# Seven block products in place of eight for half of an MLP's second projection, with weight sums made by accumulating DMAs

## The reference

```python
def squared_relu_mlp(h, w1, w2):
    return jnp.square(jax.nn.relu(h @ w1)) @ w2      # w1 2048 x 8192, w2 8192 x 2048

x = x + squared_relu_mlp(rmsnorm(x, norm_mlp[l]), w_mlp_in[l], w_mlp_out[l])
```

## Time and profile before

| | |
|---|---|
| median of 3 runs | 1684.41 us (1684.21 to 1684.99) |
| the profiled execution | 1684.11 us |
| its span, first to last instruction | 1682.3 us |
| PE busy, share of the span | 99% |
| DVE, ACT busy | 66%, 47% |
| granted TensorE clock | 1.0 |
| P2, four turns | 382.6 to 1085.9 us of the span |

### The profile page before, as it was taken

The page is one execution under the profiler, slowest core; times in us unless marked ns, Lnnn a source line. Parts: engine busy times, 40 slices in busy tenths (PEclk is TensorE's granted clock), DMA queues, the critical chain, the costliest instruction groups (busy, mean ns, idle before and its releaser), DMA issues.

```text
span 1682.3 us, 25173 instructions
## 1 busy us (share of the span) xinstructions
PE 1673.5 (99%) x9397; PEld 1453.9 (86%) x9397; DVE 1112.0 (66%) x1118; ACT 795.6 (47%) x989; POOL 55.2 (3%) x61
## 2 busy tenths in 40 slices
...
PEclk9999999999999999999999999999999999999999
...
GB/s 310 220 133 110 189 138 175 163 211 269 255 280 251 260 278 277 253 232 279 266 289 243 254 260 256 214 235 168 174 164 177 196 190 188 182 192 174 196 205 88
DMA packets 171692, 361.48 MB, mean 215 GB/s; under 512 B 11008, under 2 KB 17472, under 8 KB 171344
## 3 DMA queue, kind: packets, MB, share of 16 engines
...
q10 hardware_dynamic: 144, 0.26, 0.0%
...
## 4 chain that ended last, share of the span: by engine, by line
PE 97%; DVE 1%; issue 1%; DMA 0%; ACT 0%; SPq 0%; POOLq 0%; POOL 0%; ACTq 0%; DVEq 0%
PE G L762 31%; PE S L762 13%; PE S L776 12%; PE G L776 12%; PE G L745 10%; PE G L779 6%; PE S L779 6%; PE S L715 1%; PE G L751 1%; PE S L1147 0%; DMA raw<-in_w_in 0%; DVE window_sums L1830 0%; PE S L1140 0%; PE S L1126 0%; PE S L1014 0%
## 5 line engine op out<-in xcount | busy, mean ns | idle before, releaser
L1453 DVE TENSOR_TENSOR w_lo<-raw,w_hi 128x1024 fp32r<-128x1024 f32 (+1 forms) x573 | 704.1, 1245 | 416.5 <-ACT w_hi L1181 415.0
L1181 ACT ACTIVATE w_hi<-raw 128x1024 fp32r<-128x1024 f32 (+1 forms) x574 | 591.6, 1046 | 593.1 <-PE G L762 176.7
L762 PE MATMUL G<-w_hi,X_pair 128*128 128x512 f32 (+2 forms) x1456 | 444.5, 383 | 0.1
L762 PEld LDWEIGHTS G<-w_hi,X_pair 128*128 128x128 f32 x1456 | 269.6, 188 | 55.4 <-issue 3.3
L762 PE MATMUL G<-w_lo,X_pair 128*128 128x512 f32 (+2 forms) x728 | 276.8, 380 | 0.0
L776 PE MATMUL S<-Y_pair,w_hi 128*128 128x512 f32 x768 | 267.0, 390 | 0.0
L776 PE MATMUL G<-Y_pair,w_hi 128*128 128x512 f32 x768 | 266.8, 390 | 0.0
L779 PE MATMUL G<-Y_pair,w_lo 128*128 128x256 f32 x768 | 216.6, 282 | 0.0
L779 PE MATMUL S<-Y_pair,w_lo 128*128 128x256 f32 x768 | 216.6, 282 | 0.0
L745 PE MATMUL G<-Y_pair,w_hi 128*128 128x256 f32 x1088 | 194.0, 280 | 1.1 <-DVE Y_pair L1569 0.9
L776 PEld LDWEIGHTS S<-Y_pair,w_hi 128*128 128x128 f32 x768 | 144.2, 188 | 30.2
...
## 6 DMA issues: line engine op xcount, KB each, us to landing
raw<-in_w_in SPq DMA_DIRECT2D x142, 512.0 KB, 4.5
raw<-in_w_mlp_in SPq DMA_DIRECT2D x128, 512.0 KB, 5.3
raw<-in_w_mlp_out SPq DMA_DIRECT2D x128, 512.0 KB, 6.5
ada_w<-in_w_ada SPq DMA_DIRECT2D x64, 768.0 KB, 4.7
raw<-in_w_out SPq DMA_DIRECT2D x64, 512.0 KB, 4.4
raw<-in_w_merge SPq DMA_DIRECT2D x64, 512.0 KB, 4.2
raw<-in_w_branch_attn SPq DMA_DIRECT2D x16, 512.0 KB, 4.4
raw<-in_w_branch_pool SPq DMA_DIRECT2D x16, 512.0 KB, 6.0
```

The source lines that it names most:

```text
L762: ins = nc.tensor.matmul(token_bank(bank, tt)[:, 0:n], a[:, c0 + c, tok], w[:, s % SPLIT, c, 0:n], start=first and c == 0 and k == 0, stop ...
L1181: nc.scalar.activation(w_hi[:, s % SPLIT, :, 0:n], raw[:, k, :, 0:n], ACT.Copy).then_inc(hi_ready, 1)
L1453: nc.vector.tensor_tensor(w_lo[:, s % SPLIT, :, 0:n], raw[:, k, :, 0:n], w_hi[:, s % SPLIT, :, 0:n], ALU.subtract).then_inc(lo_ready, 1)
```

## The change

Half of the down half of each turn, the output columns 0 to 1023, is computed otherwise. The turn's 16 chunks of 128 hidden features form two sets of 8. In each set four chunks (two pairs) are multiplied by the two 512-column blocks with **seven** products of a 128-token half with 256 rows x 512 columns instead of eight (the Winograd form of Strassen's scheme), and the other four chunks as before. A set is 11 sub-blocks: V1 to V7, of 6 matmuls each, and N1A, N1B, N0A, N0B, of 12 each. The order in a set is V1, N1A, V3, N1B, V2, V5, N0A, V6, V7, N0B, V4. So a turn has 70 slots: 32 up, 22 mixed, 16 down. Sub-block 37 is V5 of the first set, 42 its V4, 48 V5 of the second set, and sub-block 54 is the first behind the sets.

The seven products need sums of activations and sums of weights.

- Activations: `sum_x` (4 DVE operations of 128 x 256), `sum_hi` (ACT), `sum_lo` (2 DVE operations of 128 x 512), once for each set.
- Weights: stage `neg{k}_{g}` is one ACT operation that writes the negative of a tile to another buffer (or to the same one), and then a DMA of POOL adds a sub-block of `w_mlp_out` from HBM onto it (`accum_op=ALU.add`). k = 1, 2, 4 form a chain: the negation of 2 starts from the landed sum 1 (semaphore `t1_in`), that of 4 from the landed sum 2 (`t2_in`). V5, V6, V7, V4 convert the sums 1, 2, 3, 4.
- The results are put together by `mixA` (ACT) and `mixB` to `mixG` (two DVE operations each) in place of `down0` and `down1`.

Besides, Relu and Square of the hidden features move from one DVE operation to two ACT operations ahead of the copy to `x_hi` (`hid` is now 3 operations of ACT); `hlo` (the former DVE part of `hid`) has a slot of its own behind it; the ada halves are in slots 0 to 33 (26 halves, thirteen rows) and 55 to 61 (three rows); `ada_fold` is cut in two; SP's part of P2 is unrolled, with 62 raw loads a turn; the sums for the last norm are taken later in the last turn.

```diff
-ADA_OPS = [0, 2, 4, 6, 7, 9, 11, 13, 14, 16, 18, 20, 21, 23, 25, 27, 28, 30, 32, 34, 35, 37, 39, 41, 42, 44, 46, 48,
-           49, 51, 53, 55]
+ADA_OPS = [0, 1, 2, 3, 4, 5, 6, 8, 10, 12, 13, 14, 16, 17, 18, 19, 20, 21, 22, 24, 26, 28, 29, 30, 32, 33,
+           55, 56, 57, 58, 60, 61]
...
+V1, N1A, V3, N1B, V2, V5, N0A, V6, V7, N0B, V4 = range(SET_SUBS)
+NEGATED = [(26, 0, 1), (28, 0, 3), (30, 0, 2), (33, 0, 4), (36, 1, 1), (38, 1, 3), (41, 1, 2), (45, 1, 4)]
...
+for _s in range(UP + SET_SUBS + V6):
...
+    for _j in range(4):
+        if _s == 8 * _j + 7:
+            stage("P2", _s, f"up{_j}", A=1, D=1)
+        if _s == 8 * _j + 8:
+            stage("P2", _s, f"hid{_j}", A=3)
+        if _s == 8 * _j + 9:
+            stage("P2", _s, f"hlo{_j}", D=1)
...
+    for _at, _g, _k in NEGATED:
+        if _s == _at:
+            stage("P2", _s, f"neg{_k}_{_g}", A=1)
...
+            def mixed(s, loop, i, j):
...
+                pe.wait_ge(lo_ready, count(s, loop, 1))
...
+                    elif k in (V1, V2, V4):
+                        ch = 8 * g + (0 if k == V1 else SUB) + c
+                        tok = slice(P, TOK) if k == V4 else slice(0, P)
+                        ins = product(PRODUCT[k], x_hi[:, ch, tok], x_lo[:, ch, tok], c)
+                    else:
+                        m = {V5: 0, V6: 1, V7: 2, V3: 3}[k]
+                        ins = product(PRODUCT[k], x_sum_hi(g, m)[:, c, :], x_sum_lo(g, m)[:, c, :], c)
...
+                elif name[:3] == "neg":
...
+                    else:
+                        act.wait_ge(t2_in, i * 32 + 16 * (g + 1))
+                        from_ = w_added(g, 2)
...
+                    nc.scalar.activation(w_added(g, k), from_, ACT.Copy, scale=-1.0).then_inc(act_side, 1)
...
                     act.wait_ge(dve_side, done("D", f"up{b}", i))
+                    nc.scalar.activation(right[:, :, :], right[:, :, :], ACT.Relu).then_inc(act_side, 1)
+                    act.wait_ge(act_side, step("A", name, 1, i))
+                    nc.scalar.activation(chunked(hid), right[:, :, :], ACT.Square).then_inc(act_side, 1)
+                    act.wait_ge(act_side, step("A", name, 2, i))
                     nc.scalar.activation(x_hi[:, 4 * b:4 * b + 4, :], chunked(hid), ACT.Copy).then_inc(act_side, 1)
...
-                    dve.wait_ge(dve_side, step("D", name, 1, i))
-                    nc.vector.scalar_tensor_tensor(chunked(hid), right[:, :, :], 0.0, right[:, :, :],
-                                                   ALU.max, ALU.mult).then_inc(dve_side, 1)
...
+            def add_to(g, k, i):
+                pool.wait_ge(act_side, done("A", f"neg{k}_{g}", i))
...
+                pool.dma_start(w_added(g, k), t["w_mlp_out"][row0:row0 + P * SUB, NW * n:NW * (n + 1)]
+                               .rearrange("(c p) n -> p c n", p=P), accum_op=ALU.add
+                               ).then_inc({1: t1_in, 2: t2_in, 3: t3_in, 4: t4_in}[k], 16)
```

More of the change, by code:

```diff
@@ L252 @@
         stage("P1", _s + 2, f"out_sq{_n}", A=2)
-for _j in range(4):
-    stage("P2", 8 * _j + 7, f"up{_j}", A=1, D=2)
-    stage("P2", 8 * _j + 8, f"hid{_j}", A=1, D=1)
-stage("P2", 34, "mlp_rms", D=3)
-for _n in range(4):
-    if _n == 3:
-        stage("P2", 58, "ada_fold", D=2)
-    if _n < 3:
-        stage("P2", 39 + 8 * _n, f"down{_n}", D=2)
+stage("P2", 3, "mlp_rms", D=3)
+for _s in range(UP + SET_SUBS + V6):
+    for _g in range(SETS):
+        if _s == 16 * _g + 9:
+            stage("P2", _s, f"sum_x{_g}", D=4)
+        if _s == 16 * _g + 10:
+            stage("P2", _s, f"sum_hi{_g}", A=1)
+        if _s == 16 * _g + 11:
+            stage("P2", _s, f"sum_lo{_g}", D=1)
+    for _j in range(4):
[5 more added lines that the diff above has]
+            stage("P2", _s, f"hlo{_j}", D=1)
+    if _s == UP + SET_SUBS + V1:
+        stage("P2", _s, "mixA", A=1)
+    for _at, _g, _k in NEGATED:
+        if _s == _at:
+            stage("P2", _s, f"neg{_k}_{_g}", A=1)
+    if _s == UP + SET_SUBS + N1B:
+        stage("P2", _s, "mixB", D=2)
+_set = UP + SET_SUBS
+stage("P2", _set + V6, "mixC", D=2)
+stage("P2", _set + V7, "mixD", D=2)
+stage("P2", _set + V4, "mixE", D=2)
+stage("P2", UP + MIXED, "mixF", D=2)
+stage("P2", UP + MIXED + 1, "mixG", D=2)
+stage("P2", 62, "ada_fold0", D=2)
+stage("P2", 63, "ada_fold1", D=2)
+stage("P2", 64, "down2", D=2)
 stage("P2", SPLIT_AT, "down3_0", P=1, D=1)
@@ L838, in loop_waits @@
                         pe.wait_ge(dve_side, step("D", "down3_1", 1, i - 1) if i else done("D", "res_T3"))
-                    if s in (16, 24, 32, 48):
-                        pe.wait_ge(dve_side, step("D", f"up{0 if s == 16 else 1 if s == 24 else 2 if s == 32 else 3}", 1, i))
-                    if b == 4 and s % 2 == 0:
-                        pe.wait_ge(dve_side, done("D", f"hid{(s % 8) // 2}", i))
+                    if s in (16, 24, UP, UP + V2):
+                        pe.wait_ge(dve_side, step("D", f"up{(16, 24, UP, UP + V2).index(s)}", 1, i))
+                    if s == UP + MIXED:
+                        pe.wait_ge(dve_side, done("D", "mixD", i))
+                    if s == UP + MIXED + 8:
+                        pe.wait_ge(dve_side, done("D", "mixG", i))
                 else:
@@ L1177, in main @@
                     return
-                act.wait_ge(raw_in[k], v if loop is None else loop[0] * (16 * loop[1] // RAW) + v)
+                r = raw_of(s, loop)
+                g, k = set_sub(s, loop)
+                if k in SET_SUMS:
+                    act.wait_ge({V5: t1_in, V6: t2_in, V7: t3_in, V4: t4_in}[k], loop[0] * 32 + 16 * (g + 1))
+                else:
+                    act.wait_ge(raw_in[r % RAW], raw_count(r, loop))
                 if s >= SPLIT:
-                    act.wait_ge(used, count(s, loop, 1 - SPLIT))
-                nc.scalar.activation(w_hi[:, s % SPLIT, :, 0:n], raw[:, k, :, 0:n], ACT.Copy).then_inc(hi_ready, 1)
+                    here = s - PHASE["P2"][0]
+                    early = in_mlp(loop) and any(k <= here < k + SPLIT - 1 for k in SKIPS_AT)
+                    act.wait_ge(used, count(s, loop, 1 - (SPLIT - 1 if early else SPLIT)))
+                nc.scalar.activation(w_hi[:, split_of(s, loop), :, 0:n], source(s, loop)[:, :, 0:n], ACT.Copy).then_inc(hi_ready, 1)
             def halves(name, dst, chunks, i=None, gain=None):
@@ L1425, in norm_sums @@
                     else:
-                        act.wait_ge(dve_side, step("D", f"down{n}", tt + 1, last) if n < 3 else step("D", f"down3_{tt}", 1, last))
+                        act.wait_ge(dve_side, done("D", "mixG", last) if n < 2 else step("D", "down2", tt + 1, last) if n < 3
+                                    else step("D", f"down3_{tt}", 1, last))
                     src = x_nf[:, tt, :] if k else x[:, tt, NW * n:NW * (n + 1)]
```

277 lines of the change are left out of this document (241 added, 36 removed).

## The result

The changed kernel takes **1715.99 us** (median of 4 runs, 1713.99 to 1716.52), the kernel before 1684.35: ratio 1.0185, 95% interval 1.0167 to 1.0203. It is slower by 31.6 us, where +5.6 was forecast (1690, range 1679 to 1704). The profiled execution took 1716.03 us, its span 1714.2, which is 31.9 over the span before.

The account below looks back on a forecast made before the run. PE was taken to bound the kernel, busy 99% at clock 1.0. 1684.1 (profiled) - 10.9 (matmuls) + 4 x 3.99 (waits) + 0.5 (hand-overs) = 1689.7; the median 0.3 higher: 1690 us, range 1679 to 1704.

Parts of the forecast that it names:

- The gain: Mixed sets of P2's down halves: 48 matmuls fewer, 10.88 us saved, 2.72 a turn.
- The wait ahead of V5: Once a turn PE waits 3.99 us for sub-block 37, since ACT's neg4_0 can't start before DVE's hlo3 ends.
- Its last leg: From the start of w_lo of sub-block 36 to V5's first product: 6.65 us in the laying-out.
- The accumulating DMAs: POOL's adding DMAs in P2: each lands 6.5 us after issue, so hidden, with little to spare.
- The allowance of 6.8 us: Second set of a turn: three landings and two negations before V4's conversion allow 6.8 us for each landing.
- The slope: Landings beyond 6.9 us: 16 us in all for each us; stated as +12 at 7.5, +20 at 8.0.
- The clock: PE's granted clock in P2: taken as 1.0, with no term for a fall.
- The last turn: Later norm sums of the last turn and the two halves of ada_fold: zero, at most 1 us once.
- `mixC` and `mixD`: They end 0.35 us before PE wants sub-block 54: no cost, but first to go when V4's sum is late.
- ada: Row loads in P2's dense part: 4.7 us each, late only from about 6.5; at 8 a turn grows by 1.2.
- the sums come late: Rival: accumulation of 7 to 8 us, or ada rows of 8, gives 1692 to 1705 us; chance 0.17.
- the doubled transfer: Rival: adding DMAs read two sources and take 11.0 us, giving 1755 us; above 1705, chance 0.10.

Follow-up runs that it names:

- e14: Changed kernel with stages respread over slots, no adding DMAs or negations: plain DMAs bring each sum's second tile, DVE subtracts the first; 1679.82 us, ratio 0.9971.
- e3: Changed kernel with plain copies in place of POOL's adding DMAs, leaving out the adding; 1710.79 us, ratio 1.0154.
- e5: Changed kernel with the negations and adding DMAs of sums 2 and 3 of the first set exchanged; 1724.54 us, ratio 1.0238.
- e11: Changed kernel with stages, POOL's DMAs and ada rows respread, plain copies for adding DMAs; 1679.80 us, against 1694.28 for the same kernel with adding.
- e4: Kernel before, with one PE wait added in each turn's down half, meant as about 4.3 us (turns 0, 2) or 2.4 us (1, 3); 1708.74 us.
- e15: e14 with norm sums in slots 56, 58, 62 instead of 56, 59, 61 and two ada halves one slot earlier; 1679.73 us, ratio 0.9973.
- e13: Changed kernel respread over slots, last turn with sums2 in slot 61, ada_fold in 64 and 66; 1694.49 us, against 1694.28 with sums2 in 62, ada_fold in 66.

## Why the prediction was wrong

The sign and the mechanism ahead of V5 were right; the time was 26 us off. Two steps failed most: the clock, put at 1.0 and so at nothing, where it took about 11 us; and the landings of the adding DMAs, put at 6.5 us each, where they took 6.0 to 13.1. Waits of PE came to 25.3 us instead of 16.5; of what lies beyond 4 x 3.99, late sums made 4.1 (2.1 ahead of V5, 2.0 near the end of the mixed part), the end of the last turn 3.3 and sub-block 36 2.0. By its own steps:

1. **The gain**: forecast 2.72 us a turn. Where nothing waits (e14), a down half takes 84.6 instead of 87.05: 2.45 us, 9.8 in all. Nearly right.
2. **The wait ahead of V5**, 3.99 forecast: 3.96 in turn 0. Its last leg holds where the order alone releases it (6.7 us in e3 and e5, 6.65 laid out). But in all four turns the adding DMA of sum 2 ended last, by 0.3 us in turn 0 and more in the others, and the wait in those was 4.48 to 5.03. Over four turns 18.0 us instead of 16.
3. **The accumulating DMAs**: this term failed. 6.5 us was the median of the 24 into `w_sum` to 0.1, but over all 32 it is 8.9, and a chain isn't made of medians. I took one price for all eight, though in the first set sum 3 is issued 3 us ahead of sum 2: they landed after 10.9 to 12.1 and 12.1 to 13.1 us. The allowance of 6.8 us was worked out for the second set alone; for the first I had not asked when sum 2 must be there. The slope was not in step either: 16 us for each us beyond 6.9 makes +15 at 7.5 and +23 at 8.0, not +12 and +20. The causes are the adding (2 to 3 us of a landing, and 14.5 us of the whole in e11) and the place behind sum 3 in the queue. I had kept the rule of the Trainium skill (page "Collectives: The Full Stack", section "The bandwidth ceiling: the fold count and why AG ≠ RS ≠ AR": a reduction reads two sources and runs at half the rate, stated there for collectives) as a rival. Its direction is borne out by e11: 9.4 against 6.5 us. The sum that I hung on it, 1755, is not: the adding didn't double the landing.
4. **The clock** was assumed at 1.0 without a word, and this was the largest miss. Taking each down half less 84.6 and less its waits leaves 3.2, 3.1, 3.3 and 6.1 us: 15.7 in all. An estimate splits it. PE worked through 23.7 of the 30.7 us at 0.5, with 0.427 us from one matmul to the next instead of 0.227, which loses 11.1 us. Each of the 13 waits costs 0.27 us that the brackets don't count (see the last section), 3.5 us. About 0.9 us of the last turn stands in e14 too. e4 shows the clock's part in the kernel before: 1.9 to 3.0 us on top of each such wait.
5. **The last turn**: "zero, at most 1 us once". It was a wait of 2.52 behind `sums2` with 3.4 us at 0.5, one of 0.79 close ahead of it, and two more of 1.08 (ahead of sub-block 36) and 0.78 (for `mixD`) in that turn.
6. **`mixC` and `mixD`** had 0.35 us of reserve and were "the first to go": PE waited 0.67 and 0.78 us for `mixD` in turns 1 and 3. Right.
7. **ada**: "late only from 6.5 us". The median is 6.4, single rows were later: row 12 took 8.0 to 9.8 us in the changed kernel, where DVE stood up to 2.2 us for it beside the other two chains, and in e3 DVE stood up to 5.2 us for it.

The balance of P2: -9.8 (gain) + 25.3 (all waits of 0.3 us and more) + 15.7 = +31.2, as measured. Since the 15.7 is what was left over, that this agrees proves nothing; the estimate in step 4 is worked out apart from it and gives 15.5. As to the rivals: "the sums come late" (0.17) was the nearest in kind, but at 1692 to 1705 without the clock. With the clock at 1.0 and a median for each landing, no case above 1705 but the doubled transfer was in my list.

What stays open: what decides when in a wait, or behind it, the clock falls (in e4 1.66 us ahead of the end of one wait of 4.30 us and 0.59 behind that of the other), and why some waits up to 3.72 us brought no fall; the 4.7 us that the last down half of e14 loses, of which 3.3 are waits behind conversions and neither the place of the norm sums (e15) nor of `ada_fold` (e13) is shown to be the cause; and how much of the 7 us that sum 2 loses by its place is sum 3 ahead of it and how much SP's loads beside it.
